# Idle products among the meta queries' values, a reordered norm prologue, and the delta rule's updates by transposes

## The chip, the core and the metric

The kernel runs on one core of a Trainium2 chip. The time is that of one execution on the device, in microseconds (us). The engines are PE (TensorE; PEld is its weight load), DVE (VectorE), ACT (ScalarE), POOL (GpSimd) and SP, which issues most DMAs. Each engine runs its own list of instructions in order; semaphores make one wait for another.

## What is computed

A sequence of 16 meta tokens and 512 real tokens, width 1024, passes through two blocks. In the first block, layer 0 mixes with differential attention (4 heads) and dense attention (8 heads), and layer 1 with windowed attention. The second block drops the meta tokens and has two layers, each with an mLSTM branch, a gated delta rule branch, LayerNorm and a SwiGLU feed-forward part. Of the reference, cut to what the change touches:

```
# block 1, layer 0: the 16 meta queries are a block of their own
o = einsum('bhqs,bhsv->bqhv', softmax(q_meta k) ..., v)

# block 2, delta rule, for each head and chunk of 64 tokens
a_low = where(strict, beta_i * (k_i . k_j) * decay_ij, 0)
u, w  = solve(I + a_low, [v * beta, k * beta * exp(gcum)])

# block 2, layer: LayerNorm over the 1024 features, twice
x = layernorm(alpha * x + mix, ln1_g, ln1_b)
x = layernorm(alpha * x + ffn, ln2_g, ln2_b)
```

## The kernel before, in words

The program is a sequence of stages, each with its own lists for the engines and a barrier behind it. Tokens lie in the free dimension (512 wide), features in the partitions, 8 chunks of 128 features (`KC`). Weights come from HBM in f32 and are split into a rounded high part (ACT, L557) and the remainder (DVE, L690 and, for the first slot in four pieces, L870); the dense products (L441) are made of three products of such parts, all in f32r.

Three places matter here.

**The meta queries' values** (`query_values`, L1208 to L1224, in the attention stage `attA`). When the probabilities of the 16 meta queries have been turned, PE multiplies them with the values in six batches: four of heads whose values are 128 wide, two of pairs of heads 64 wide. Each product has only 16 (or 32) columns. ACT then copies `mix` (L1329), and the ordinary heads go on.

**The norm** (`Normed`, L218 to L309), used five times: at the head of stage `mqkv` in both layers of block 2, at the head of `ffn` in both, and once at the very end (`store`). PE spreads the mean over all partitions (L240), ACT copies it to SBUF (L270), DVE subtracts it from chunk 0 of the activations `h` (L277), POOL from chunks 1 to 7 (L282). DVE scales each chunk (L291), ACT makes its high part (L296), DVE its low part (L299), ACT finishes `h` (L302); PE's first product block (48 products with 512 columns: 8 chunks by 6) follows the chunks as they come. Between the products of the norm PE makes idle ones (`keep_busy`, L101): products of the identity whose result nobody reads, two instructions each. The second weight slot is split while the chunks pass: its high part on ACT after chunk 3, its low part on DVE (L690, 128x2048) after the scale of chunk 5.

The end of a stage that feeds a norm: DVE adds tile 7's residual (L778), adds it to the sum (L753), ACT squares it (L608), DVE adds the squares (L745). PE makes 12 idle products meanwhile (L538), and a barrier ends the stage.

**The delta rule** (`delta_rule`, L2531 is `each`: four products 128x128 in eight instructions; `turn` is four transposes). Two streams (e = 0 and 1) of four heads' chunks run interleaved, in four pairs. The triangular system is inverted by levels b = 1 to 5 with a last quarter-sized one. In a level PE makes y = nb t (bank 0), ACT copies y (L2671), PE makes w = y u (bank 2) and z = uᵀ y (bank 1), and DVE updates both u (L2756, in `room` for stream 0) and its transpose t (L2751). For pairs 0 to 2 the levels also carry pieces of the next pair's preparation (`prepare` on PE, `prepared` on DVE, decays on ACT at L2656 and L2658).

## Time and profile before

| | |
|---|---|
| median of 3 runs | 3865.29 us (3865.06 to 3866.74) |
| the profiled execution: its time, its span | 3866.34 us, 3864.5 us |
| PE busy | 3732.8 us, 97% |
| DVE, ACT, POOL busy | 48%, 31%, 5% |
| mean granted clock of TensorE | 0.98 |

Time and span differ by 1.8 us, which lies around the first and the last instruction. PE is busy nearly always, but "busy" counts idle products, and it counts an instruction's whole time at the lower clock too. In a row of windows each engine has its busy time and its instructions in brackets (PE, PEld, DVE, ACT, POOL), then come TensorE's granted clock as a share of 2.4 GHz, the DMA share and GB/s. In a timeline a row stands for a run of like instructions: start, duration of the run, engine, line, operands, count, and in square brackets the idle time before it and what ended that.

### The profile page before, as it was taken

To read this page: it belongs to the slowest core of one execution; us is meant where nothing else is said; L and a number is where in the kernel's file an instruction comes from. 1 tells how busy PE (TensorE), PEld (TensorE's weight loads), DVE (VectorE), ACT (ScalarE), POOL (GpSimd) and SP (SyncE) were. 2 spreads that over 40 slices of the span, in tenths; PEclk is the share of its full clock that TensorE was granted. 3 is DMA by queue.
4 is the path that set the end of the run, shared out by engine and by line. 5 is a ranking of instruction groups with operands and counts; after the bars stand their busy time and mean duration, and the time that the engine had idled before them with its cause. 6 is when DMAs were issued, how large, how long until landed. Compare 5 with 4: busy or idle time off the path is not lost. (4 is left out here: it accounts for less than half of the span.)

```text
span 3864.5 us, 51800 instructions
## 1 busy us (share of the span) xinstructions
PE 3732.8 (97%) x21089; PEld 3132.3 (81%) x21089; DVE 1860.2 (48%) x2531; ACT 1202.8 (31%) x1762; POOL 197.4 (5%) x216
## 2 busy tenths in 40 slices
PE   8899999999999999999999999999999999999998
PEld 8759999977888787878888788878687788887887
DVE  6475434345534435366554633353536655464334
ACT  3353222244222333232232322234423223323222
POOL 0000000000000100001210100010000122000000
PEclk9899999999999999999999999999999999999999
DMA  3102222212222211220002222221122000222222
GB/s 124 55 2 81 94 88 88 77 54 79 103 90 96 77 55 66 87 87 23 1 28 98 77 92 100 88 82 66 55 97 78 33 1 11 105 77 95 96 91 89
DMA packets 49926, 278.74 MB, mean 72 GB/s; under 512 B 10237, under 2 KB 12797, under 8 KB 20538
## 3 DMA queue, kind: packets, MB, share of 16 engines
q1 hardware_dynamic: 48684, 274.29, 19.8%
q8 instruction: 149, 2.44, 0.2%
q10 hardware_dynamic: 1038, 1.56, 0.1%
q14 instruction: 55, 0.45, 0.0%
HBM read 273.57 MB, written 2.22 MB: 71 GB/s over the span
## 5 line engine op out<-in xcount | busy, mean ns | idle before, releaser
L441 PE MATMUL ps<-xs,ffn_w 128*128 128x512 f32 x2112 | 483.1, 390 | 6.4 <-DVE xs L299 3.8
L441 PEld LDWEIGHTS ps<-xs,ffn_w 128*128 128x128 f32 x2112 | 395.5, 188 | 93.2 <-DVE xs L299 8.4
L441 PE MATMUL ps<-u,mlp_w 128*128 128x264 f32 (+1 forms) x2880 | 454.2, 321 | 0.2 <-DVE u L878 0.2
L441 PEld LDWEIGHTS ps<-u,mlp_w 128*128 128x128 f32 x2880 | 415.9, 189 | 37.6 <-issue 0.3
L441 PE MATMUL ps<-hn,mlp_w 128*128 128x264 f32 (+1 forms) x2304 | 363.6, 320 | 0.0
L441 PEld LDWEIGHTS ps<-hn,mlp_w 128*128 128x128 f32 x2304 | 332.4, 188 | 30.3 <-issue 0.5
L441 PE MATMUL ps<-xs,cv_w 128*128 128x512 f32 x1152 | 268.7, 394 | 0.0
L441 PEld LDWEIGHTS ps<-xs,cv_w 128*128 128x128 f32 x1152 | 215.2, 188 | 59.6 <-issue 13.7
L441 PE MATMUL ps<-ff,ffn_w 128*128 128x512 f32 x1056 | 241.2, 390 | 0.0
L441 PEld LDWEIGHTS ps<-ff,ffn_w 128*128 128x128 f32 x1056 | 198.3, 188 | 41.9 <-issue 1.0
L557 ACT CAST ffn_w<-raw 128x2048 fp32r<-128x2048 f32 (+1 forms) x74 | 124.2, 1678 | 304.0 <-PE ps L441 264.0
L690 DVE TENSOR_TENSOR mlp_w<-raw,mlp_w 128x2048 fp32r<-128x2048 f32 x70 | 160.5, 2292 | 114.7 <-ACT mlp_w L557 114.7
L441 PE MATMUL ps<-hn,qk_w 128*128 128x264 f32 x1344 | 176.7, 294 | 10.2 <-DVE qk L805 10.2
L441 PEld LDWEIGHTS ps<-hn,qk_w 128*128 128x128 f32 x1344 | 172.7, 196 | 13.3 <-issue 12.7
L557 ACT CAST mlp_w<-raw 128x2048 fp32r<-128x2048 f32 x70 | 132.7, 1895 | 155.5 <-PE ps L441 125.4
L441 PE MATMUL ps<-xs,branch_b_w 128*128 128x512 f32 x768 | 180.0, 396 | 0.0
L441 PE MATMUL ps<-xs,branch_a_w 128*128 128x512 f32 x768 | 178.1, 394 | 0.0
L441 PE MATMUL ps<-hbs,branch_b_w 128*128 128x512 f32 x768 | 176.0, 391 | 0.0
L441 PEld LDWEIGHTS ps<-xs,branch_b_w 128*128 128x128 f32 x768 | 146.1, 191 | 32.5 <-issue 2.2
L441 PEld LDWEIGHTS ps<-xs,branch_a_w 128*128 128x128 f32 x768 | 145.3, 189 | 31.8
L441 PEld LDWEIGHTS ps<-hbs,branch_b_w 128*128 128x128 f32 x768 | 144.3, 188 | 30.7 <-issue 1.0
L690 DVE TENSOR_TENSOR ffn_w<-raw,ffn_w 128x2048 fp32r<-128x2048 f32 (+1 forms) x74 | 148.0, 2000 | 41.9 <-ACT ffn_w L557 41.7
(451 smaller groups left out, 5223.0 us busy)
## 6 DMA issues: line engine op xcount, KB each, us to landing
raw<-in_w_ffn_up SPq DMA_DIRECT2D x44, 1024.0 KB, 4.8
raw<-in_w_up SPq DMA_DIRECT2D x32, 1024.0 KB, 4.8
raw<-in_w_down SPq DMA_DIRECT2D x32, 1024.0 KB, 4.7
raw<-in_w_conv SPq DMA_DIRECT2D x24, 1024.0 KB, 4.8
raw<-in_w_ffn_down SPq DMA_DIRECT2D x32, 704.0 KB, 4.1
raw<-in_w_mqk SPq DMA_DIRECT2D x10, 1024.0 KB, 4.8
raw<-in_w_qk_even SPq DMA_DIRECT2D x9, 1024.0 KB, 4.8
raw<-in_w_mv SPq DMA_DIRECT2D x8, 1024.0 KB, 4.8
```

Source lines behind the costliest of these rows:

```text
L441: ins = nc.tensor.matmul(bank(u)[:, h, :], w[:, s, wp, k * g.bw + j * P:k * g.bw + (j + 1) * P], g.xs[:, xp, k, h * n:(h + 1) * n], start= ...
L557: nc.scalar.copy(w[:, s, 0, 0:g.kc * g.bw], ws.raw[:, s, 0:g.kc * g.bw]).then_inc(g.s["high_done"], 1)
L690: nc.vector.tensor_tensor(w[:, s, 1, 0:g.kc * g.bw], ws.raw[:, s, 0:g.kc * g.bw], w[:, s, 0, 0:g.kc * g.bw].bitcast(F32), ALU.subtract).th ...
```

## The change

Eight edits. (1) Normed takes `first`: DVE subtracts the mean from chunks 0 to first-1 and POOL from the rest; first is 3 for the four norms in the layers and 4 for the last. Three idle products between the mean's spread and the wait for `inverted` go. (2) The second slot's high part goes on ACT ahead of chunk 0, its low part on DVE behind chunk 7's low part. (3) At a stage's end with statistics 14 idle products instead of 12. (4) There, ACT's square of tile t waits for one sum fewer. (5) There, DVE adds the square of tile t-1 ahead of its wait for tile t. (6) Two idle products ahead of each of the six batches of `query_values`. (7) In the delta rule the four products z = uᵀy go; PE turns the updated u into the same bank by four transposes, and DVE copies it to t. (8) With it the order within a level: on PE both y, [preparation A], both w, turn A, [preparation B], turn B; on DVE both u, both t, then both prepared pieces.

```diff
--- before.py
+++ after.py
@@ -218,7 +218,9 @@
 
 
 
-    def __init__(self, nc, ps, x, stats, mean, gain, bias, eps, ident):
+
+    def __init__(self, nc, ps, x, stats, mean, gain, bias, eps, ident, first=3):
+        self.first = first
         self.nc, self.ps, self.x, self.stats, self.mean = nc, ps, x, stats, mean
         self.gain, self.bias, self.eps, self.ident = gain, bias, eps, ident
 
@@ -244,7 +246,6 @@
         by_tokens(6, self.stats.sumsq, s["squared"])
         pe.wait_ge(s["m_done"], 1)
         spread(5, self.m, s["m_spread"])
-        keep_busy(nc, ps[:, 3, :], self.ident, 3)
         pe.wait_ge(s["inverted"], 1)
         spread(7, self.r, s["r_spread"])
         keep_busy(nc, ps[:, 3, :], self.ident, 6)
@@ -274,20 +275,22 @@
         dve.wait_ge(s["rooted"], 1)
         nc.vector.reciprocal(self.r[:, :], self.r[:, :]).then_inc(s["inverted"], 1)
         dve.wait_ge(s["m_copied"], 1)
-        nc.vector.tensor_tensor(self.x[:, 0, :], self.x[:, 0, :], self.mean, ALU.subtract).then_inc(s["centred"], 1)
+        for c in range(self.first):
+            nc.vector.tensor_tensor(self.x[:, c, :], self.x[:, c, :], self.mean, ALU.subtract).then_inc(s["centred"], 1)
 
     def gpsimd(self, pool):
         pool.wait_ge(self.s["m_copied"], 1)
-        for c in range(1, KC):
+        for c in range(self.first, KC):
             self.nc.gpsimd.tensor_tensor(self.x[:, c, :], self.x[:, c, :], self.mean, ALU.subtract).then_inc(self.s["centred_p"], 1)
 
     def scale(self, dve, c):
         s = self.s
         if c == 0:
             dve.wait_ge(s["r_spread"], 1)
-            dve.wait_ge(s["centred"], 1)
+        if c < self.first:
+            dve.wait_ge(s["centred"], c + 1)
         else:
-            dve.wait_ge(s["centred_p"], c)
+            dve.wait_ge(s["centred_p"], c - self.first + 1)
         self.nc.vector.scalar_tensor_tensor(self.x[:, c, :], self.x[:, c, :], self.gain[:, c:c + 1], self.ps[:, 7, :],
                                             ALU.mult, ALU.mult).then_inc(s["scaled"], 1)
 
@@ -535,7 +538,7 @@
                 if ws.mat is not None:
                     no = last.t0 + last.tiles + last.extra
                     pe.wait_ge(freed, no + 1)
-                    keep_busy(nc, bank(no % tiles)[:, 0, :], ws.mat, 6 if last.stats is None else 12)
+                    keep_busy(nc, bank(no % tiles)[:, 0, :], ws.mat, 6 if last.stats is None else 14)
 
             @block.scalar
             def _(act):
@@ -604,7 +607,7 @@
                     else:
                         act.wait_ge(freed, tiles + tile_no(g, t, t >= g.tpb) + 1)
                     if t >= 2:
-                        act.wait_ge(g.s["summed"], t - 1)
+                        act.wait_ge(g.s["summed"], max(1, t - 2))
                     nc.scalar.activation(sq[:, t % 2, :], g.dst[:, t, :], ACT.Square).then_inc(g.s["squared"], 1)
 
                 def shift(g):
@@ -653,13 +656,12 @@
                             nc.scalar.activation(sq[:, c % 2, :], whole[:, c, :], ACT.Square).then_inc(x_squared, 1)
                 if normed is not None:
                     normed.roots(act)
+                    high(g, 1, 1)
                     for c in range(KC):
                         normed.high(act, c, g.xs[:, 0, c, :], x_high)
                         if c:
                             act.wait_ge(x_low, c)
                             normed.finish(act, c - 1)
-                        if c == 3:
-                            high(g, 1, 1)
                     act.wait_ge(x_low, KC)
                     normed.finish(act, KC - 1)
                 if beside is not None:
@@ -769,6 +771,8 @@
                 def summed_tile(g, t, pos, j):
                     u, no = slot_of(g, pos, j), tile_no(g, t, t >= g.tpb)
                     shifted = g.stats.shift is not None
+                    if t >= 2:
+                        sum_square(g, t - 1)
                     dve.wait_ge(filled, 1 + no + 1)
                     if shifted and t >= g.tpb:
                         dve.wait_ge(g.s["readied"], t - g.tpb + 1)
@@ -784,8 +788,6 @@
                         add_up(g, t)
                         if t + g.tpb < g.tiles:
                             ready(g, t + g.tpb)
-                    if t >= 2:
-                        sum_square(g, t - 1)
 
                 def tile(g, t, pos, j):
                     u = slot_of(g, pos, j)
@@ -895,9 +897,8 @@
                         normed.scale(dve, c)
                         if c:
                             normed_low(c - 1)
-                        if c == 5:
-                            low(g, 1, 1)
                     normed_low(KC - 1)
+                    low(g, 1, 1)
                 if beside is not None:
                     beside.vector(dve, -1)
                 for i, g in enumerate(gemms):
@@ -1211,6 +1212,7 @@
                     batches += [(n_diff + 2 * g, 2, HD, 1, HD * g, jobs[n_diff + 2 * g][3]) for g in range(2)]
                     for i, count, width, n, col, off in batches:
                         cols = slice(META * i, META * (i + count))
+                        keep_busy(nc, ps[:, 7, 2 * P:4 * P], ident, 2)
                         for j in range(NU + 1):
                             for e in range(1 if diff[i] else 2):
                                 rows = slice(width * e, width * e + width)
@@ -2583,6 +2585,10 @@
                     pe.wait_ge(s["o_copied"], i + 1)
                     nc.tensor.matmul(ps[0:GH, 4 * e + 3, :], pick[:, 2 * i + e, :], f["sq"][:, :], start=True, stop=True).then_inc(s["picked"], 1)
 
+                def turn_update(i, b, e, f, s):
+                    pe.wait_ge(s["u_done"], levels * i + b + 1)
+                    turn(e, 1, f["u"], s["z_filled"])
+
                 for n in range(levels):
                     for e, f, s in both:
                         prepare(0, n, e, f, s)
@@ -2615,9 +2621,12 @@
                                     quarter(e, 2, f["y"], f["u"], s["w_filled"])
                                 else:
                                     each(e, 2, f["y"], f["u"], s["w_filled"])
-                                    each(e, 1, f["u"], f["y"], s["z_filled"])
+                        if 0 < b < levels - 1:
+                            turn_update(i, b, *both[0])
                         if i + 1 < pairs:
                             prepare(i + 1, b, *both[1])
+                        if 0 < b < levels - 1:
+                            turn_update(i, b, *both[1])
                     for e, f, s in both:
                         pe.wait_ge(s["kbe_done"], i + 1)
                         pe.wait_ge(s["u_done"], levels * (i + 1))
@@ -2742,21 +2751,20 @@
                         for e, f, s in both:
                             prepared(i + 1, 0, e, f, s)
                     for b in range(1, levels):
-                        if i + 1 < pairs:
-                            prepared(i + 1, b, *both[0])
                         for e, f, s in both:
                             dve.wait_ge(s["w_filled"], (levels - 1) * i + b)
-                            if b < levels - 1:
-                                dve.wait_ge(s["z_filled"], (levels - 2) * i + b)
-                                nc.vector.tensor_tensor(f["t"][:, :, :], f["t"][:, :, :], bank(e, 1), ALU.subtract).then_inc(s["t_done"], 1)
                             if b == levels - 1:
                                 upper = f["u"][0:HC, :, HC:CHUNK]
                                 ins = nc.vector.tensor_tensor(upper, upper, bank(e, 2)[0:HC, :, HC:CHUNK], ALU.subtract)
                             else:
                                 ins = nc.vector.tensor_tensor(f["u"][:, :, :], f["u"][:, :, :], bank(e, 2), ALU.subtract)
                             ins.then_inc(s["u_done"], 1)
+                        for e, f, s in both if b < levels - 1 else ():
+                            dve.wait_ge(s["z_filled"], (levels - 2) * i + b)
+                            nc.vector.tensor_copy(f["t"][:, :, :], bank(e, 1)).then_inc(s["t_done"], 1)
                         if i + 1 < pairs:
-                            prepared(i + 1, b, *both[1])
+                            for e, f, s in both:
+                                prepared(i + 1, b, e, f, s)
                     for c in range(NCH - 1):
                         for e, f, s in both:
                             dve.wait_ge(s["s_filled"], (NCH - 1) * i + c + 1)
@@ -2776,8 +2784,8 @@
     shifted = Stats(stats.total, stats.sumsq, mean, ones)
     g_rows = sums[0:GH, :, 0:SEQ]
 
-    def normed(gain, bias, eps):
-        return Normed(nc, ps, x, stats, mean, par[:, gain:gain + KC], par[:, bias:bias + KC], par[:, eps:eps + 1], ident)
+    def normed(gain, bias, eps, first=3):
+        return Normed(nc, ps, x, stats, mean, par[:, gain:gain + KC], par[:, bias:bias + KC], par[:, eps:eps + 1], ident, first)
 
     with ExitStack() as ctx:
         with nc.Fori(0, LAYERS2) as layer:
@@ -2835,7 +2843,7 @@
                                           dense("dn1", ff, per // P, D, "add", dst=x, stats=shifted)], whole=x, normed=norm_1,
                       beside=NextParameters(par[:, :], a["par2"][bass.ds(layer + 1, 1), :, :].rearrange("a p n -> (a p) n"), norm_1))
             settle(nc)
-    return normed(IN_G, IN_B, IN_EPS)
+    return normed(IN_G, IN_B, IN_EPS, 4)
 
 
 def second_constants():
```

On PE, in the stage `attA`, at the meta queries' values (`attA_ptq` holds their turned probabilities, `v` the values; `mats` is the identity's tensor). Before:

```order
L1184 MATMUL ps<-mats,attA_prob 128x128 x4
L1136 MATMUL ps<-qk 128x264 x4
L1221 MATMUL ps<-attA_ptq,v 128x16 x4
L1221 MATMUL ps<-attA_ptq_meta,v 128x16
L1221 MATMUL ps<-attA_ptq,v 128x16 x4
L1221 MATMUL ps<-attA_ptq_meta,v 128x16
```

After:

```order
L1185 MATMUL ps<-mats,attA_prob 128x128 x4
L1137 MATMUL ps<-qk 128x264 x4
L101 MATMUL ps<-mats 128x128 x2
L1223 MATMUL ps<-attA_ptq,v 128x16 x4
L1223 MATMUL ps<-attA_ptq_meta,v 128x16
L101 MATMUL ps<-mats 128x128 x2
L1223 MATMUL ps<-attA_ptq,v 128x16 x4
L1223 MATMUL ps<-attA_ptq_meta,v 128x16
```

Two products of 128 columns now stand ahead of each batch of ten instructions (this list counts a product once where the trace has two instructions).

On DVE, in the norm of stage `mqkv` (the stage `ffn` reads alike), before:

```order
L275 RECIPROCAL mqkv_n_r<-mqkv_n_r 128x4
L277 TENSOR_TENSOR h<-h,room 128x512
L870 TENSOR_TENSOR mqkv_w<-raw,mqkv_w 128x512
L291 SCALAR_TENSOR_TENSOR h<-h,room,ps 128x512 x2
L299 SCALAR_TENSOR_TENSOR xs<-h,room,xs 128x512
...
L690 TENSOR_TENSOR mqkv_w<-raw,mqkv_w 128x2048
L291 SCALAR_TENSOR_TENSOR h<-h,room,ps 128x512
L299 SCALAR_TENSOR_TENSOR xs<-h,room,xs 128x512
```

After (both lists leave out scales and low parts of the chunks between, which alternate as those shown):

```order
L276 RECIPROCAL mqkv_n_r<-mqkv_n_r 128x4
L279 TENSOR_TENSOR h<-h,room 128x512 x3
L872 TENSOR_TENSOR mqkv_w<-raw,mqkv_w 128x512
L294 SCALAR_TENSOR_TENSOR h<-h,room,ps 128x512 x2
L302 SCALAR_TENSOR_TENSOR xs<-h,room,xs 128x512
...
L294 SCALAR_TENSOR_TENSOR h<-h,room,ps 128x512
L302 SCALAR_TENSOR_TENSOR xs<-h,room,xs 128x512 x2
L692 TENSOR_TENSOR mqkv_w<-raw,mqkv_w 128x2048
```

Two subtractions have moved ahead of the first scale, and the 128x2048 remainder has moved from among the chunks to behind them.

On PE, in the delta rule, one level of a pair that carries preparation (`room` and `delta_y` are u and y, `delta_t` and `delta_nb` t and nb), before:

```order
L2531 MATMUL ps<-delta_t,delta_nb 128x128 x8
L2549 MATMUL ps<-rows,sel 128x512 x2
L2531 MATMUL ps<-room,delta_y 128x128 x4
L2531 MATMUL ps<-delta_y,room 128x128 x4
L2531 MATMUL ps<-room,delta_y 128x128 x4
L2531 MATMUL ps<-delta_y,room 128x128 x4
L2549 MATMUL ps<-rows,sel 128x512 x2
```

After:

```order
L2533 MATMUL ps<-delta_t,delta_nb 128x128 x8
L2551 MATMUL ps<-rows,sel 128x512 x2
L2533 MATMUL ps<-room,delta_y 128x128 x8
L2546 MATMUL ps<-mats,room 128x128 x4
L2551 MATMUL ps<-rows,sel 128x512 x2
L2546 MATMUL ps<-mats,room 128x128 x4
```

Eight products have become eight transposes, one half ahead of preparation B and one behind it, and the transposes read the u that DVE has just written.

## Rows read from the trace of the kernel before

**Rows 1.** The page's head: busy time and share of the span.
```profile
PE 3732.8 (97%) x21089; PEld 3132.3 (81%) x21089; DVE 1860.2 (48%) x2531; ACT 1202.8 (31%) x1762; POOL 197.4 (5%) x216
```

**Rows 2.** Windows around the meta queries' values.
```profile
174.00:178.00 4.00, 4.00 (x32) 3.35 (x31) 3.21 (x10) 2.08 (x5) 0.20 (x1) 1.00 0.01 1
178.00:180.00 2.00, 2.00 (x14) 1.91 (x14) 0.94 (x2) 0.00 (x0) 0.20 (x1) 0.78 0.74 230
186.00:192.00 6.00, 6.00 (x15) 3.47 (x16) 0.00 (x0) 1.37 (x5) 0.00 (x0) 0.50 0.01 3
```

**Rows 3.** Timeline there: the batches on PE, and what DVE waits for.
```profile
175.52 1.07 PE L1221 MATMUL ps<-attA_ptq,v 128*128 128x16 f32 x8
...
176.84 1.07 PE L1221 MATMUL ps<-attA_ptq,v 128*128 128x16 f32 x8
...
179.68 1.89 PE L1221 MATMUL ps<-attA_ptq,v 128*128 128x16 f32 x8
...
193.88 0.71 DVE L1408 CUSTOM_DVE_ANT_0 attA_prob<-ps,attA_bias 128x528 f32<-128x528 f32 x1 [14.91 <-PE ps L1136]
```

**Rows 4.** Timeline, the norm at the head of `ffn`, first layer of block 2.
```profile
2201.25 0.69 DVE L277 TENSOR_TENSOR h<-h,room 128x512 f32<-128x512 f32 x1 [1.68 <-ACT room L270]
2201.30 6.40 POOL L282 TENSOR_TENSOR h<-h,room 128x512 f32<-128x512 f32 x4 [196.73 <-ACT room L270]
2201.86 1.77 DVE L870 TENSOR_TENSOR ffn_w<-raw,ffn_w 128x512 fp32r<-128x512 f32 x1
...
2203.55 1.39 DVE L291 SCALAR_TENSOR_TENSOR h<-h,room,ps 128x512 f32<-128x512 f32 x2
...
2205.19 1.17 PE L441 MATMUL ps<-xs,ffn_w 128*128 128x512 f32 x4 [0.39 <-ACT xs L296]
```

**Rows 5.** Line L282 over all five norms: duration ns min/median/max.
```profile
L282 POOL TENSOR_TENSOR h<-h,room x35: 1256/1737/1794, 1312.7 to 3858.6; 128x512 f32<-128x512 f32 x35
```

**Rows 6.** Busy time by stretch: end of stage to norm, `ffn`'s first product block, `mqkv`'s.
```profile
2193.00:2196.40 3.40, 0.90 (x9) 0.74 (x8) 1.22 (x2) 1.52 (x4) 0.00 (x0) 1.00 0.00 0
2196.50:2203.00 6.50, 6.50 (x32) 6.50 (x32) 3.50 (x9) 1.78 (x4) 1.70 (x1) 0.50 0.01 3
2205.00:2221.00 16.00, 12.93 (x49) 8.83 (x50) 13.58 (x15) 12.07 (x18) 7.80 (x5) 1.00 0.34 131
1321.00:1336.00 15.00, 15.00 (x53) 9.58 (x52) 9.14 (x11) 10.50 (x15) 3.75 (x3) 1.00 0.20 71
```

**Rows 7.** Timeline of DVE in the last norm, `store`.
```profile
3850.65 0.69 DVE L277 TENSOR_TENSOR h<-h,room 128x512 f32<-128x512 f32 x1 [1.60 <-ACT room L270]
3852.54 2.06 DVE L291 SCALAR_TENSOR_TENSOR h<-h,room,ps 128x512 f32<-128x512 f32 x3 [1.19 <-PE ps L240]
...
3859.89 0.75 DVE L291 SCALAR_TENSOR_TENSOR h<-h,room,ps 128x512 f32<-128x512 f32 x1 [0.48 <-POOL h L282]
```

**Rows 8.** Timeline at the end of the stage ahead of `ffn`.
```profile
2190.39 2.84 PE L101 MATMUL ps<-mats 128*128 128x128 f32 x24
...
2192.71 0.63 ACT L608 ACTIVATE branch_b_tmp<-h 128x512 f32<-128x512 f32 x1 [4.82 <-DVE sums L745]
2193.37 0.69 DVE L745 TENSOR_TENSOR sums<-sums,branch_b_tmp 128x512 f32<-128x512 f32 x1 [0.76 <-ACT branch_b_tmp L608]
```

**Rows 9.** Timeline, delta rule: a level of the last pair.
```profile
1964.41 0.97 PEld L2531 LDWEIGHTS ps<-delta_t,delta_nb 128*128 128x128 f32 x8
...
1966.48 0.97 PEld L2531 LDWEIGHTS ps<-room,delta_y 128*128 128x128 f32 x8
...
1968.65 0.69 DVE L2751 TENSOR_TENSOR delta_t<-delta_t,ps 128x512 f32<-128x512 f32 x1 [2.57 <-PE ps L2531]
...
1970.06 0.97 PEld L2531 LDWEIGHTS ps<-delta_t,delta_nb 128*128 128x128 f32 x8
```

**Rows 10.** Timeline, delta rule: two successive levels of the first pair.
```profile
1805.58 0.52 PEld L2531 LDWEIGHTS ps<-delta_t,delta_nb 128*128 128x128 f32 x4 [0.36 <-issue]
...
1812.63 0.74 PEld L2531 LDWEIGHTS ps<-delta_t,delta_nb 128*128 128x128 f32 x6 [0.36 <-issue]
```

## The prediction

> **What bounds the kernel now.** I read the page's head first: PE is busy 97% of the span and the next engine, DVE, 48% [rows 1]. So a microsecond of PE work that goes is worth one only where PE is really fed at that place, and a microsecond of idle products costs one unless PE would have waited. The page can't tell which, so I went to each place of the change in the timeline and in windows. At the meta queries' values DVE sits idle for 14.91 us, until the product it needs has come through PE's list [rows 3]: there PE alone sets the end, and the granted clock falls from 1.00 to 0.50 (2.4 to 1.2 GHz) on the way [rows 2]. In `mqkv` PE is fully busy behind the norm, 15.00 of 15.00 us, while `ffn`'s first block leaves 3.07 of 16 us idle (12.93 busy) [rows 6]. In the delta rule PE is nearly full too, but its steps hang on one another through DVE and ACT [rows 9]. In the last norm nothing but DVE, POOL and ACT works [rows 7].
>
> **The meta queries' values (edit 6).** Twelve idle products are added where PE sets the end. At a stage's end twelve of them take 2.84 us at full clock [rows 8], so a pair is 0.47 us, and at half clock I take double, as the eight instructions of a batch grow from 1.07 to 1.89 us [rows 3]. The question is whether the clock still falls. Before, it fell in the window from 178 to 180 (0.78 granted: full for some 1.1 us of it, thus until about 179.1), 3.6 us after the first batch had started at 175.52 [rows 2, 3], although PE is counted busy all the time. What PE did were products of 16 columns. The new stretch has 8 instructions of 16 columns, two more, and now four of 128 columns in every 1.32 + 0.47 = 1.79 us; a batch starts every 1.32 us now (175.52, 176.84) [rows 3]. The idle products are a quarter of the time, and between them the array streams as little as before. No row shows such a mixture. I take it that the clock falls at the same time, since three quarters of the stretch are unchanged. Two batches then run at full clock and four at half: 2 x 0.47 + 4 x 0.95 = 4.7, less 0.2 because the clock may come back a little sooner: **+4.5 us**. Bounds: if the clock never fell, the pairs would cost 2.8 and the half-clock stretch would be saved. From 179.1 to some 193 us it is 14 us long, but much of that is PE waiting for ACT or being bound by weight loads; doubling shows as 0.8 us in the eight instructions of a batch [rows 3], and I put the whole saving at about 4.7 us from six such pieces. That bound is -1.9; the other is +5.7, all six pairs at half clock.
>
> **The norm's prologue (edits 1 and 2).** This is the costliest part. In `ffn` DVE subtracts chunk 0 at 2201.25; POOL's first subtraction is queued at 2201.30. DVE's next instruction, L870, has two inputs in SBUF, as the subtraction has. It takes 1.77 us where a subtraction alone takes 0.69 [rows 4], because POOL's instruction went in ahead of it. POOL's own take 1.737 us in the median but 1.256 at best [rows 5]. So the two engines alternate, one instruction each, and each further DVE instruction of this kind costs about 1.72 us as long as POOL has work. DVE was ready at 2201.86, before the end of its own subtraction, and still came second [rows 4]: being next in its own list does not help it. Now three of them stand ahead of the first scale where there was one (L870) behind the subtraction: two more, 2 x 1.72 = 3.44 us. The first scale moves from 2203.55 to about 2206.99, the first product from 2205.19 to about 2208.6. The Trainium skill has this as a rule, in "SBUF — State Buffer", section "SBUF: two separate sides": a DVE instruction with two SBUF inputs and a GpSimd instruction that reads SBUF lock the port pair against each other for the whole instruction, and the other fully blocks. By that rule the change is a loss at this point, and the trace agrees (1.77 against 0.69).
>
> What hides it? In `mqkv` PE is full behind the first chunks, so the delay stands, less some 0.3 us of small waits that vanish: 3.1 us, twice, **+6.2**. In `ffn` the first block's 48 products have 3.07 us of slack (49 instructions by 2221, so the next block starts at about 2220.8) [rows 6]; moreover L690 (2.3 us) leaves the series of chunks. Counted through: scale 0 at +5.74 us from the first subtraction, eight chunks at 1.4 us in the mean (POOL is finished after about five), then 2.3 for L690: the second block may start at +19.6, against 2220.8 - 2201.25 = 19.6 before [rows 4, 6]. That is **+0.3** for both. In the last norm the fourth subtraction ends after 0.69 + 3 x 1.72 = 5.85, eight scales at 0.66 follow, and the last one starts at 3850.65 + 5.8 + 4.6 = 3861.04 instead of 3859.89 [rows 7]: **+1.15**, and ACT's last instruction follows as before. Three idle products less and the earlier spread of `r` are worth nothing, since DVE is now later than `r`. ACT's early high part of slot 1 (1.9 us) lies in ACT's wait for the first scale.
>
> A second cost is the clock. Where PE was busy 0.90 of 3.40 us, the windows behind it show 0.50 [rows 6]. In the new prologue PE has nothing between its last idle product (2204 to 2205) and 2208.6, a gap of about 4 us, where it was under 0.4 [rows 4]. If the clock falls, the first chunks' six products, some 1.4 us a chunk at full clock, take 2.7, against DVE's 1.7 a chunk: 1 us lost on each of one or two chunks. I take 1.5 us for each `mqkv` and 0.5 for each `ffn`, whose slack is partly used: **+4.0**, bounds 0 and +6.
>
> **The delta rule (edits 7 and 8).** The z products of a stream are as long as its w, 1966.48 to 1967.38, 0.90 us, so both streams' are 1.8 us a level [rows 9]. Four transposes are half as many instructions, 0.47 a stream by the 24 that took 2.84 [rows 8]. Were PE the bound without waits, 40 levels (20 per layer, each of both streams) would give 40 x 0.9 = 36 us. But z needs no fresh u: it used y and the old one. The transposes need the new u. The chain of a level of the last pair is then, from w's start: DVE starts on u 1.27 later (as L2751 at 1968.65 behind the products at 1967.38) and takes 0.69 [rows 9]; turn starts about 0.12 after it; the copy of t could start some 0.8 after that (1.27 less half of the eight instructions), but DVE is at the other stream's u until about +2.85; 0.69 for the copy, and with 0.12 again y starts at about +3.65. From y to w it is 1.92 (2.07 in these rows, 1964.41 to 1966.48, of which 0.15 is PE's wait for the other stream's t) [rows 9]. That gives a period of 5.57 us against 1970.06 - 1964.41 = 5.65 [rows 9]: 0.1 saved of 0.9. With preparation the period is 7.05 [rows 10]; there PE has other work in the waits, which is for the change, but the prepared pieces now come behind both t on DVE, the decays on ACT behind them, and ACT's copy of the next y queues behind the decays. Laying the five levels out with these durations I get -0.6, -0.4, +0.7, -0.4, -0.2 and +0.6 at the quarter level, where PE waits for DVE: -0.25 a pair. Three pairs and -0.4 to -0.7 for the last: -1.45 a layer, **-2.9 us** in all. Bounds: -22 us (0.75 saved at each of the 30 prepared levels, if ACT's queue is harmless) and +6 (the wait of +0.7 at two more levels of each of the six prepared pairs would be +8; the last pair's gain off that).
>
> **The stages' ends (edits 3 to 5).** DVE's last sum runs from 2193.37 to 2194.06 and gates the barrier; PE's idle products end at 2193.23 [rows 8]. ACT's last square at 2192.71 waited for the sum before it; freed, it starts about 1.3 us sooner and DVE ends at about 2192.75. But PE now makes 14 idle products and ends at 2193.23 + 0.47 = 2193.70. Gain 0.36 at four ends; at the fifth, ahead of block 2, where other DVE work closes the stage with PE near it, I count 0.3 lost: **-1.1**.
>
> **The sum.** 4.5 + 6.2 + 0.3 + 1.15 + 4.0 - 2.9 - 1.1 = +12.2 on the profiled run's 3866.34 us: 3878.5. The median of the runs shown is 1.05 lower, so the forecast against it is 3877.4, some 0.3% slower.
>
> **The rivals.** What a measurement of this kernel can tell from no change is about 0.2%, 7.7 us: faster is under 3857.6, slower over 3873.0. The forecast's own case, with the clock in the norms' gaps at its bounds (+8 to +14), gives 3873 to 3880: chance 0.58, of which 0.06 falls below 3873.
>
> (A) DVE keeps its turn over consecutive subtractions, and POOL comes only after them. Then scale 0 comes at about +2.5 instead of +2.3, POOL has fewer chunks to do, and L690's stall in `ffn` goes: at most 3.07 us in each `ffn`, I count 2.5, and 1.5 in `store`, nothing in `mqkv`. The norms give -6.5 instead of +11.65, the sum is -6.0, 3859.3. For it: nothing but that POOL's wait here ended 0.05 after DVE's. Against: L870 is just such a consecutive instruction and lost its turn [rows 4]. 0.08.
>
> (B) The idle products hold the clock at the meta queries' values: -1.9 instead of +4.5, 3871.0, just inside no change. For it: they are the only wide products there. 0.12.
>
> (C) The delta rule follows PE's work, not the chain: -22 instead of -2.9 gives 3858, with a little more or with (B) it is faster than 3857.6. This is the rival on the other side. It decides once a prepared level is shorter than 7.05 by over 0.75 us. For it: PE is nearly full there; against: the chain of the last pair, which is 5.57 by the same rows. 0.12.
>
> (D) The delta rule gets slower by the queue of decays on ACT, +6: 3886. 0.10.
>
> Slower: 0.52 + 0.01 + 0.04 + 0.10 = 0.67, lowered to 0.63 as several small terms are estimates; faster 0.03 from (A), 0.07 from (C): 0.10; the same 0.27. The range from 3860 to 3885 leaves out (D)'s end and the larger half of (C).
>
> **What would show it.** In the norms: two of the three L279 at about 1.7 us instead of 0.69, the first L441 of each norm 3.4 us later against the first subtraction, a granted clock under 1.00 just behind it; if the subtractions take 0.69 each, (A) holds. At the meta queries: L101 pairs of 0.47 and then 0.95 us, and the window around 186 to 192 still at 0.50; at 1.00, (B) holds. In the delta rule: y of one level to y of the next, 5.6 and about 7.0 us; 6.3 speaks for (C). At the ends: L608's last square right behind L778, and the barrier behind PE. The prediction is wrong above all if PE's work sets the delta rule's pace, or if the alternation with POOL is another thing than I read.

## The result, and the profile after

The changed kernel takes 3876.6 us (median of 8 runs, 3872.5 to 3880.49) against 3866.15 us of the kernel before (8 runs, 3864.14 to 3870.77): ratio 1.0027, interval [1.0017, 1.0036]. It is slower by 0.27%; the forecast was 3877.4 us, 0.3%. The profiled execution took 3879.14 us with a span of 3877.3, 12.8 us longer than before's.

PE is counted less busy than before [rows 1], since the delta rule lost products, and yet the span is longer. The page's head after:

```profile
PE 3725.1 (96%) x20783; PEld 3114.4 (80%) x20783; DVE 1875.2 (48%) x2542; ACT 1201.0 (31%) x1762; POOL 181.0 (5%) x205
```

**The meta queries' values.** Windows, then the timeline of the same place:

```profile
174.00:178.00 4.00, 3.75 (x28) 3.13 (x29) 3.36 (x10) 1.96 (x5) 0.20 (x1) 1.00 0.00 0
178.00:180.00 2.00, 2.00 (x18) 1.94 (x17) 1.16 (x3) 0.12 (x2) 0.20 (x1) 0.96 0.74 197
186.00:192.00 6.00, 4.99 (x49) 4.25 (x49) 0.00 (x0) 1.32 (x11) 0.00 (x0) 0.50 0.01 3
```

```profile
179.44 0.91 PE L101 MATMUL ps<-mats 128*128 128x128 f32 x4
180.15 1.73 PE L1223 MATMUL ps<-attA_ptq,v 128*128 128x16 f32 x8
...
182.34 1.22 PE L101 MATMUL ps<-mats 128*128 128x128 f32 x4
...
198.92 0.71 DVE L1410 CUSTOM_DVE_ANT_0 attA_prob<-ps,attA_bias 128x528 f32<-128x528 f32 x1 [19.54 <-PE ps L1137]
```

The reader sees the clock fall at the third pair, as it fell in the third to fourth batch before [rows 2, 3], and the later pairs at half clock (1.22 us with the last one's end). DVE's work starts at 198.92 where it started at 193.88: 5.0 us later. Of this 0.4 us was there ahead of the batches: counted from the products of `attA_prob` in front of them (on PE, L1184 at 173.85 before, L1185 at 174.25 after), the stretch takes 24.7 us instead of 20.0, so the edit costs 4.6 us. In the nine further traces that have no idle products here the stretch takes 20.1 us six times and 18.5 us three times.

**The norm**, in `ffn` of the first layer, to set against [rows 4]; behind it the line of the moved subtractions over all norms:

```profile
2206.98 4.05 DVE L279 TENSOR_TENSOR h<-h,room 128x512 f32<-128x512 f32 x3 [1.68 <-ACT room L271]
2207.02 8.04 POOL L284 TENSOR_TENSOR h<-h,room 128x512 f32<-128x512 f32 x5 [195.98 <-ACT room L271]
...
2210.95 1.75 DVE L872 TENSOR_TENSOR ffn_w<-raw,ffn_w 128x512 fp32r<-128x512 f32 x1
2212.62 1.39 DVE L294 SCALAR_TENSOR_TENSOR h<-h,room,ps 128x512 f32<-128x512 f32 x2
...
2214.26 1.19 PE L444 MATMUL ps<-xs,ffn_w 128*128 128x512 f32 x2 [5.16 <-ACT xs L299]
```

```profile
L279 DVE TENSOR_TENSOR h<-h,room x16: 693/1746/1779, 1321.3 to 3866.3; 128x512 f32<-128x512 f32 x16
```

Three subtractions take 4.05 us, the first 0.69 and the others 1.75. The first scale stands 5.64 us behind the first subtraction, where it was 2.30 [rows 4]. PE waits 5.16 us for its first product, and the granted clock falls on top: 0.81 from 2203.9 to 2213.

**The last norm**, DVE, against [rows 7]:

```profile
3862.35 5.71 DVE L279 TENSOR_TENSOR h<-h,room 128x512 f32<-128x512 f32 x4 [1.83 <-ACT room L271]
3867.98 5.34 DVE L294 SCALAR_TENSOR_TENSOR h<-h,room,ps 128x512 f32<-128x512 f32 x8
```

From the first subtraction to the end of the last scale it is 10.97 us now, and 3860.64 - 3850.65 = 9.99 before: +1.0.

**The end of a stage**, against [rows 8]:

```profile
2197.39 3.29 PE L101 MATMUL ps<-mats 128*128 128x128 f32 x28
...
2198.32 0.63 ACT L611 ACTIVATE branch_b_tmp<-h 128x512 f32<-128x512 f32 x1 [4.82 <-DVE h L782]
2198.32 0.69 DVE L755 TENSOR_TENSOR sums<-sums,h 128x512 f32<-128x512 f32 x1
2198.98 0.69 DVE L747 TENSOR_TENSOR sums<-sums,branch_b_tmp 128x512 f32<-128x512 f32 x1
```

ACT's square starts right behind the residual; DVE is through at 2199.67, and now PE's idle products, until 2200.68, gate the barrier.

**The delta rule**, a level of the last pair, against [rows 9]:

```profile
1972.83 2.02 PE L2533 MATMUL ps<-delta_t,delta_nb 128*128 128x128 f32 x16
...
1974.69 2.00 PE L2533 MATMUL ps<-room,delta_y 128*128 128x128 f32 x16
...
1976.57 0.66 PE L2546 MATMUL ps<-mats,room 128*128 128x128 f32 x4
...
1978.16 2.02 PE L2533 MATMUL ps<-delta_t,delta_nb 128*128 128x128 f32 x16
```

The period is 5.33 us (before 5.65).

In a pair that carries preparation the starts of y on PE are now 6.31, 6.42, 7.57, 6.56 and 5.77 us apart (before 7.05, 7.05, 7.25, 7.15 and 6.33; the fifth step leads to the quarter-sized level). In the long one PE waits for ACT's copy of y, which stands behind the decays on ACT. In the quarter-sized level (its y at 1895.87) it waits for DVE:

```profile
1879.77 2.05 PE L2533 MATMUL ps<-room,delta_y 128*128 128x128 f32 x16 [0.41 <-ACT delta_y L2680]
...
1895.87 0.67 PE L2541 MATMUL ps<-delta_t,delta_big_n 64*64 64x64 f32 x8
...
1897.99 0.63 PE L2546 MATMUL ps<-mats,qkv 128*128 128x128 f32 x4 [0.61 <-DVE qkv L2725]
...
1900.12 1.95 PE L2533 MATMUL ps<-room,qkv 128*128 128x128 f32 x16
```

The same level before, in the second layer:

```profile
3156.70 1.16 PE L2539 MATMUL ps<-delta_t,delta_big_n 64*64 64x64 f32 x16
...
3159.99 2.02 PE L2531 MATMUL ps<-room,qkv 128*128 128x128 f32 x16
```

**Where the 12.8 us arose.** Starts of the same work on PE in the two traces, and how much later each is after the change:

| mark | before | after | later by |
|---|---|---|---|
| behind the meta queries' values | 192.34 | 197.57 | 5.2 |
| first scores of layer 1's attention, block 1 | 812.41 | 817.28 | 4.9 |
| norm of `mqkv` | 1309.12 | 1317.44 | 8.3 |
| second product block of `mqkv` | 1335.33 | 1348.52 | 13.2 |
| `branch_a` | 1483.37 | 1493.53 | 10.1 |
| delta rule | 1773.55 | 1784.16 | 10.6 |
| `branch_b` | 2008.75 | 2015.23 | 6.5 |
| norm of `ffn` | 2195.72 | 2202.32 | 6.6 |
| `ffn`, way down | 2329.60 | 2335.69 | 6.1 |
| norm of `mqkv`, layer 2 | 2580.59 | 2586.79 | 6.2 |
| past `mqkv`, layer 2 | 2642.50 | 2652.40 | 9.9 |
| delta rule, layer 2 | 3043.14 | 3055.43 | 12.3 |
| `branch_b`, layer 2 | 3278.21 | 3288.94 | 10.7 |
| last norm | 3846.36 | 3856.21 | 9.8 |
| end | 3864.5 | 3877.3 | 12.8 |

Most steps are those of the forecast, but three are not, all in stages that nothing touches: +3.4 us between 812 and 1309, -3.1 ahead of the first `branch_a`, and +2.4 between `mqkv` and the delta rule of layer 2. The first of these places in windows, after and (last row) before:

```profile
908.00:914.00 6.00, 5.51 (x32) 3.19 (x34) 0.51 (x3) 0.58 (x1) 0.00 (x0) 0.72 0.01 3
914.00:922.00 8.00, 5.62 (x27) 4.58 (x22) 5.77 (x10) 5.73 (x12) 0.10 (x1) 0.79 0.00 0
```

```profile
908.00:915.00 7.00, 4.87 (x26) 4.14 (x27) 5.26 (x10) 5.61 (x11) 0.10 (x1) 1.00 0.00 0
```

PE's work is the same; the granted clock isn't. The runs that follow ask whether that is chance.

### The profile page after: what moved, and what is told of

Same layout as the page of the kernel before. It is cut to its first block and busy times, and to the rows that moved or that the text cites. A ratio compares the mean times of both kernels' runs of the same rounds, so it can differ in the third digit from the quotient of the medians.

```text
span 3877.3 us, 51108 instructions
## 1 busy us (share of the span) xinstructions
PE 3725.1 (96%) x20783; PEld 3114.4 (80%) x20783; DVE 1875.2 (48%) x2542; ACT 1201.0 (31%) x1762; POOL 181.0 (5%) x205
## 3 DMA queue, kind: packets, MB, share of 16 engines
q8 instruction: 147, 2.41, 0.3%
## 5 line engine op out<-in xcount | busy, mean ns | idle before, releaser
L856 DVE TENSOR_TENSOR ffn_res<-ffn_tmp,ps 128x512 f32<-128x512 f32 x44 | 30.3, 689 | 280.3 <-PE ps L444 276.1
```

The costliest lines, as they stand in the source:

```text
L856: nc.vector.tensor_tensor(res[:, v, :, :], tmp[:, v, :, :], bank(slot_of(g, pos, 1)), ALU.mult).then_inc(freed, 2)
```

## The experiments

All ratios are to runs of the kernel before on the same chip. The experiments ran on several chips, where the median of the kernel before was 3865.97 to 3869.45 us, so two experiments are compared by their ratios. Where a figure is given by stage, it is the difference of starts in the traces, as in the table above.

**1. The changed kernel without the idle products** (edit 6 undone).

```diff
-                        keep_busy(nc, ps[:, 7, 2 * P:4 * P], ident, 2)
```

> The changed kernel without the idle products among the meta queries' values (edit 6 undone). In the traces of before and after, DVE's first work behind these values starts at 193.88 and at 198.92 us: 5.0 us later with the change. If the idle products alone did that, the start is back at 193.9 within 0.3 us, the granted clock between 180 and 192 is 0.50 as before, and the whole is 5 us faster than the changed kernel, about 3872. Rival: another edit or the run moved it, and the start stays near 199.

3868.17 us (10 runs), ratio 1.0004 [0.9995, 1.0014]. PE's work behind the values starts at 192.66 (before 192.34, after 197.57). So the idle products are the 5 us there. But the whole is 8.4 us under the change's median (by the ratios 9), more than the 5 expected: the 3.4 us between 812 and 1309 are gone too (0.2 in this trace).

**2. The further subtractions alone** on the kernel before.

```diff
-        nc.vector.tensor_tensor(self.x[:, 0, :], self.x[:, 0, :], self.mean, ALU.subtract).then_inc(s["centred"], 1)
+        for c in range(self.first):
+            nc.vector.tensor_tensor(self.x[:, c, :], self.x[:, c, :], self.mean, ALU.subtract).then_inc(s["centred"], 1)
...
-        for c in range(1, KC):
+        for c in range(self.first, KC):
```

> The kernel before with the two (in the last norm three) further subtractions on DVE and nothing else: the idle products of the norm and the place of the second slot's split stay as they were. Forecast's theory, alternation with POOL: two of three subtractions take about 1.7 us, the first product of each norm comes 3.4 us later against the first subtraction, and the whole is slower by more than the change's own norms were, since L690 still stands among the chunks: mqkv +4 each, ffn +3 each, store +1.2, so +13 to +17, about 3881. Rival (A), DVE keeps its turn: subtractions of 0.69 us each and no more than +2. A third theory: the second slot's place is worth nothing, then ffn is within 1 us of before and the whole is +10.

3883.98 us (4 runs), ratio 1.0045 [1.0028, 1.0062]: slower than the change as a whole. First products 3.3 us late in `mqkv` and in `ffn`, and of these `ffn` keeps 2.5 by its way down. What holds it is the 128x2048 split still in the midst of the chunks, in DVE's timeline:

```profile
2217.91 0.75 DVE L303 SCALAR_TENSOR_TENSOR xs<-h,room,xs 128x512 fp32r<-128x512 f32 x1 [1.23 <-ACT xs L300]
2218.58 2.28 DVE L694 TENSOR_TENSOR ffn_w<-raw,ffn_w 128x2048 fp32r<-128x2048 f32 x1
2220.78 0.74 DVE L295 SCALAR_TENSOR_TENSOR h<-h,room,ps 128x512 f32<-128x512 f32 x1
```

**3. The delta rule's change alone** (edits 7 and 8).

> The kernel before with the delta rule's change alone (edits 7 and 8). In the trace after, each prepared pair is 1.3 us shorter than before wherever the clock was the same, and a level of the last pair 0.31 us. Theory 1, the chain through u, the turn and t sets the level: the same figures, so 5 to 6 us a layer where no clock fall comes in between, and 3855 to 3860 for the whole. Theory 2, the lighter work of PE lets the clock fall more often in the delta rule (after: 3.4 us at half clock in several places where before had one), and it takes the gain back: more windows below 1.00 than before in both layers, and a whole of 3862 to 3866. Theory 3, PE's work sets the pace: 0.9 us per level, 3830.

3863.24 us (10 runs), ratio 0.9989 [0.998, 0.9999]. The time is in theory 2's range; against this chip's kernel before, 3867.91, it is 4.7 us less, between theories 1 and 2. The first layer gives 1.4 us, the second 4.4, and from the second level of a pair on the levels are the same in both: the starts of y follow one another by 6.43, 7.57, 6.56 and 5.77 us where they did by 7.05, 7.25, 7.15 and 6.33. Theory 3 (PE's work) is out.

What differs between the layers is the clock, at the pairs' ends and in their first levels. From the quarter-sized level to the next pair's first y it is 19.75 us at full clock and 21.3 with a fall (18.85 before); the first level of a pair grows by 1.6 or 3.1 us where the clock falls in it. In this trace the falls make 6.2 us in the first layer and 3.1 in the second, where a layer of the kernel before has 1.6. Three windows of this kernel: inside the first pair's first level, a pair's end in the second layer with a fall, and one without:

```profile
1796.00:1799.00 3.00, 3.00 (x11) 2.12 (x11) 0.00 (x0) 0.59 (x1) 1.44 (x2) 0.50 0.02 5
3096.00:3118.00 22.00, 19.84 (x147) 16.18 (x146) 12.85 (x24) 5.91 (x16) 5.05 (x4) 0.92 0.00 1
3204.00:3222.00 18.00, 16.73 (x142) 14.07 (x142) 10.56 (x20) 5.91 (x16) 4.54 (x4) 1.00 0.00 1
```

Put together from pieces at full clock alone (an estimate), a layer takes 182.7 us from the first y to the last quarter-sized level, against 188.2 before: 5.4 us less. So each theory has its share: the chain gives theory 1's 5 to 6 us a layer, and theory 2's falls take part of it back.

**4. The stages' ends alone** (edits 3 to 5).

> The kernel before with the stages' ends alone (edits 3 to 5: 14 idle products, ACT's square and DVE's sum freed of one another). Theory: at four ends DVE is finished 1.3 us sooner and PE's idle products, 0.45 us longer, now gate the barrier, so each end gives 0.4 us, the fifth loses 0.3: -1.3 in all, no change that the times can tell (3863 to 3867). Rival: DVE still gates, and nothing moves at all. Second rival: the barrier waits for something else (ACT or a DMA), then the next stage's first instruction stands where it did although DVE and PE ended otherwise.

3866.05 us (10 runs), ratio 0.9999 [0.9989, 1.0008]: no difference that the times tell. By stage: -0.4, -0.1, -0.4 and -0.3 at the four ends, as computed for all but one. Neither rival holds where the 0.4 is seen; the end with -0.1 doesn't tell.

**5. The change without its two losing parts**: no idle products among the values, one subtraction on DVE as before; the second slot's move, the ends and the delta rule as changed.

> The changed kernel without its two losing parts: no idle products among the meta queries' values, and the mean subtracted from chunk 0 alone on DVE, as before (the norm's three idle products stand too). The second slot's place, the stages' ends and the delta rule are as changed. From the other traces, stage by stage: delta rule alone -4.4 us a layer where the clock is the same (-8.8, of which falls of the clock took 3 in the first layer), the ends -0.4 each (-1.2), and in ffn, where the further subtractions without the second slot's move ended at -0.8 behind a first product at +3.3, and with it at -3.0 behind +2.6, the move gives about 2 to 2.5 each. Sum -12 to -14: 3854 to 3858 against 3867.9. Rival: the move of the second slot is worth something only behind a delayed start (DVE then has the slot's split hidden anyway), so -8 to -10.

3854.01 us (6 runs), ratio 0.9967 [0.9955, 0.9979]: 0.33% faster than before, 12.0 us at the medians, at the near edge of the -12 to -14 expected. `ffn` gives 2.0 us in each layer without any subtraction moved, so the rival (the move pays only behind a late start) is out. In DVE's timeline the split stands behind the last chunk, and PE no longer waits for it:

```profile
2211.93 1.62 DVE L299 SCALAR_TENSOR_TENSOR xs<-h,room,xs 128x512 fp32r<-128x512 f32 x2
2213.47 2.28 DVE L689 TENSOR_TENSOR ffn_w<-raw,ffn_w 128x2048 fp32r<-128x2048 f32 x1
```

**6 and 7. Three and four idle products** ahead of each batch, in the kernel before.

```diff
+                        keep_busy(nc, ps[:, 7, 2 * P:4 * P], ident, 3)
```

> The kernel before with three idle products ahead of each of the six batches instead of none. At full clock they are 18 x 0.223 = 4.0 us. Forecast's theory, the clock falls as long as the narrow products take most of the time: with three wide ones in some 2 us of a batch it still falls, and the first ordinary work of DVE behind the values starts 7 us later than before. Rival (B) in a milder form: three are enough, the granted clock stays at 1.00 through the batches, and the start is within 1 us of before (+4.0 for the products, -4.7 for the stretch at half clock).

> The same with four: 24 x 0.223 = 5.4 us at full clock. If the clock now holds, DVE's first ordinary work behind the values starts at about +0.7 against before, and the windows from 180 to 188 show 1.00. If it falls all the same, at +9 to +10. With two (the change) it fell and the start was at +5.0.

Three: 3871.52 us (8 runs), ratio 1.001 [1.0, 1.002]; the window from 180 to 184 has a granted clock of 0.54, and DVE starts at 202.32, 8.4 us late (7.6 counted from the products ahead of the batches). Four: 3876.01 us (8 runs, 3866.79 to 3881.52), ratio 1.0024 [1.0013, 1.0035]. In its trace, one of the faster executions, the clock stands at full speed through the batches and falls behind them:

```profile
180.00:184.00 4.00, 4.00 (x36) 3.92 (x35) 0.00 (x0) 0.00 (x0) 0.00 (x0) 1.00 0.01 4
184.00:186.00 2.00, 2.00 (x30) 1.81 (x30) 0.00 (x0) 0.00 (x0) 0.00 (x0) 1.00 0.00 0
186.00:192.00 6.00, 4.99 (x36) 2.83 (x35) 0.00 (x0) 2.13 (x12) 0.00 (x0) 0.79 0.00 0
```

DVE starts at 197.09, 3.2 us late instead of 0.7 (3.4 counted from the products ahead of the batches): behind the batches, where PE waits 1.0 us for ACT's `mix`, the clock falls after all. So enough idle products can hold the clock through the batches, and it doesn't pay. This is shown for one execution alone. The other seven spread from 3866.79 to 3881.52, four of them over 3878, and the median is 10 us above this chip's kernel before; whether the clock held in those isn't shown.

**8. One idle product ahead of each wait for the updated u**, on the delta change alone.

```diff
                 def turn_update(i, b, e, f, s):
+                    keep_busy(nc, bank(e, 1)[:, 0, :], ident, 1)
                     pe.wait_ge(s["u_done"], levels * i + b + 1)
```

> The kernel before with the delta rule's change and one idle product ahead of each wait for the updated u (80 a layer's pair of streams all told, 160 in the kernel of 0.22 us), where PE waits 0.2 to 0.45 us anyway. It tells whether the half-clock stretches in the delta rule after the change come from PE's lighter work. Theory 2: they vanish (none in the prepared pairs of either layer) and both layers show -4 against before, 3860 or a little under. Rival: the stretches stand as they are, since the waits are only half filled, and every idle product that is longer than its wait costs: 0 to -2 against before. Third: the idle products never fit, the chain grows by 0.1 us a level, and it is slower than the delta change alone by 4.

3865.42 us (10 runs), ratio 0.9997 [0.9988, 1.0006]; the delta change alone has 0.9989, about 3 us less, but the intervals overlap. The windows from 1830 to 1970, first of this kernel, then of the delta change alone:

```profile
1830.00:1970.00 140.00, 133.87 (x1070) 117.41 (x1069) 80.46 (x133) 38.62 (x92) 40.50 (x33) 1.00 0.00 1
```

```profile
1830.00:1970.00 140.00, 132.81 (x1026) 114.73 (x1025) 80.65 (x135) 39.35 (x94) 42.82 (x34) 0.98 0.00 1
```

The clock now holds, as theory 2 said: neither layer has a fall between its first y and its last quarter-sized level. But a prepared level takes 6.80 us instead of 6.43, and a layer gains only 2.0 to 2.2. The lighter load is what lets the clock fall, for with PE's waits filled all falls are gone. Filling costs 5.6 us a layer (188.3 us against the 182.7 at full clock of experiment 3). The falls that it removes make 1.6 to 6.4 us in the sixteen layers of the eight other traces with this change, 4.7 in the mean: some 1 us less than the filling.

**9. No POOL in the norm**: experiment 1's kernel, with the later subtractions on DVE too, each just ahead of its scale.

```diff
-        for c in range(self.first, KC):
+        for c in range(self.first, KC) if not self.own else ():
...
+        if self.own and c >= self.first:
+            self.nc.vector.tensor_tensor(self.x[:, c, :], self.x[:, c, :], self.mean, ALU.subtract).then_inc(s["centred"], 1)
```

> The changed kernel without the idle products among the meta queries' values (as in the run that undid edit 6), and with all of the mean's subtractions on DVE: the first three (four) in a row as in the change, each later one just ahead of its chunk's scale. POOL does none. It tells whether the 1.7 us a subtraction are the two engines' alternation. Theory: with POOL silent each subtraction takes 0.69 and L872's last piece too, the first scale starts 2.6 us behind the first subtraction instead of 5.7, and the first product of the norm comes at +0.3 against before instead of +3.3 in mqkv. A chunk on DVE is then subtraction, scale and low part, about 1.95 us, less than the 2.25 of PE in mqkv, so mqkv ends at about before's time; in ffn (1.36 us of PE a chunk) DVE sets the pace. Whole: about 3 to 4 us a mqkv less than its sister's 3868.2, so some 3861. Rival: the subtractions are slow for another reason (the length of the list, an operand's place), and stay at 1.7.

3856.98 us (5 runs), ratio 0.9969 [0.9956, 0.9982]; its sister, experiment 1, has 1.0004. That is 11 us at the medians and 13 to 14 by the ratios, more than expected: `mqkv` takes 1.0 us less than before in each layer, where the sister takes 4.9 and 3.7 more. DVE's timeline in `mqkv`:

```profile
1311.38 1.90 DVE L279 TENSOR_TENSOR h<-h,room 128x512 f32<-128x512 f32 x3 [0.72 <-ACT room L271]
1313.19 0.69 DVE L874 TENSOR_TENSOR mqkv_w<-raw,mqkv_w 128x512 fp32r<-128x512 f32 x1
1313.79 1.40 DVE L296 SCALAR_TENSOR_TENSOR h<-h,room,ps 128x512 f32<-128x512 f32 x2
```

The same three subtractions in the same list take 1.90 us instead of 4.05, and the first scale comes after 2.41 us instead of 5.6. This settles it: what made them slow is POOL's own work, not their place.

**10. `mqkv` alone without POOL**, on the kernel of experiment 5, one subtraction ahead.

> The kernel of the run without first and idle products (3854.0, the fastest so far), and in mqkv's norms alone every subtraction on DVE, one ahead of the first scale and each later one ahead of its own. Theory: L870's last piece takes 0.69 instead of 1.77, the first product starts 1.1 us sooner and PE, which is full behind it, passes that on: -1.1 in each mqkv, 3852. Rival: a chunk of 1.95 us on DVE is too slow when PE asks for one in 1.4 (the gates' products come only with the second chunk), and the gain is lost again by the third chunk: no difference.

3854.61 us (6 runs, 3844.81 to 3859.69), ratio 0.9968 [0.9956, 0.998]: no difference to experiment 5, but in the first layer not for the rival's reason. DVE was through early and then waited for PE's spread of r, which stands behind the norm's three idle products:

```profile
1313.40 0.75 DVE L297 SCALAR_TENSOR_TENSOR h<-h,room,ps 128x512 f32<-128x512 f32 x1 [1.06 <-PE ps L242]
```

The traced execution is the fastest of all here, 3844.81 us, 9.8 us under its kernel's median. Against experiment 5's trace it gains 4 us between `mqkv` and the first delta rule and 5.8 in that delta rule, where the two kernels are the same and the falls of the clock are not.

**11. The same without those idle products in `mqkv`.**

> The kernel of the run in which mqkv's subtractions are all on DVE, without the norm's three idle products there. In that run the first scale waited 1.06 us for PE's spread of r, which came behind the idle products at half clock, so the last piece's faster end brought nothing: the median stayed at 3854.6 against 3854.0. Theory: with them gone (they stay in ffn and store) the spread comes about 0.9 us sooner and the first scale 1.1 us behind its former place, the first product of mqkv at -1.1 against the kernel before, passed on in full: 1 us each layer, 3852.5. Rival: PE's longer idle stretch costs as much by the clock, and the median stays at 3854.

3853.69 us (6 runs), ratio 0.9965 [0.9953, 0.9977]. The first scale stands at 1311.38, 1.40 us behind the subtraction at 1309.98. Per stage `mqkv` gives 1.0 and 1.2 us, but the median is within a microsecond of experiment 5's: the mechanism is shown, the gain in time is not.

**12. The changed kernel once more.**

> The changed kernel once more, unchanged. In its first trace some 3.3 us arose between 818 and 922 us, in stages that the change does not touch, with granted clocks of 0.81 and 0.90 where the other traces show 1.00 but for one short stretch. If these fall by where an execution happens to stand, the second trace has them elsewhere or not at all, and the stages touched show the same differences as in the first: +5 at the meta queries' values, +3.3 at each first product of mqkv. If the shift of 5 us at the meta queries' values brings them on, the second trace shows them again.

3877.64 us (6 runs), ratio 1.0025 [1.0013, 1.0037]. Between 812 and 1309 the second trace again shows +3.5 us, with falls of the clock at the same two places. The kernels whose work stands there at before's time or up to 3.0 us earlier show 0.0 to 0.4, and the one with three idle products, which stands there 8.4 us later, shows 0.3. So it isn't chance from run to run: both traces with a shift of 4.9 and 6.3 us at this place have these falls, and none of the eleven traces of other kernels has the loss. As far as these traces tell, it isn't the size of the shift that costs but where it sets the later stages. Which moment decides was not tried.

## Why the prediction was right

**The meta queries' values.** Forecast +4.5, measured 5.0 at DVE's start, of which 0.4 was there before: 4.6 in both traces of the changed kernel, with two pairs at full clock and four at half. Rival (B), that the idle products hold the clock, is out for two and three products a batch. With four its mechanism is true, in the one trace, but its price is not: it still costs 3.4 us. The price of the edit is over 8 us all the same: to the 5.0 on the spot come 3.4 in untouched stages, which the forecast did not have.

**The norm's prologue.** The reading that POOL and DVE alternate stood: 1.75 us a subtraction (forecast 1.72), first product +3.3 us (3.4), +4.9 and +3.7 us for the two `mqkv` with the clock (4.6 each), and experiment 9 took the cause away. Rival (A) is out: it gave 3859.3 and 0.69 us a subtraction. The rule of the Trainium skill ("SBUF — State Buffer", "SBUF: two separate sides"), that a DVE instruction with two SBUF inputs and a GpSimd instruction that reads SBUF lock each other out for the whole instruction, agrees with 1.75 us here and 0.69 with POOL silent.

In `ffn` the sum was mis-sized: +0.3 and +1.0 for the clock in both together, measured -0.6 (-0.5 and -0.1) in the profiled pair, and -0.5 and +1.2 in the changed kernel's second trace. The terms that I wrote down, 5.74 + 8 x 1.4 + 2.3, add up to 19.2 and not to 19.6. The move of the split gives back all of the delay, though PE starts 2.5 and 2.8 us late against the stage's own start. By itself that move is worth 2.0 us a layer (experiment 5), which I had used up against the delay and not named as a gain of its own.

In the last norm +1.15 was forecast; the profiled pair has +3.0 from its start to the end, of which the norm on DVE is 1.0. The other 1.9 us arise ahead of the first subtraction, which stands 4.28 us behind the stage's start before and 6.14 after, with a granted clock of 0.90 and 0.50 in the first 2 us. This part moves from trace to trace, from 4.06 to 6.14 us: experiments 3 and 4, whose last norm is that of before, have 6.13 and 6.14, experiment 5 has 4.61, and the changed kernel's second trace 4.66. So it is the state of the clock at that moment and not the change; the change's part is +1.0.

**The delta rule.** The chain sets the pace, as forecast, and not PE's work: rival (C) needed over 0.75 us a prepared level, and the five levels of a pair give 0.4 in the mean. The size was off: -2.9 forecast, -4.1 and -1.6 in the two layers of the profiled pair, and 2.4 to 11.0 us gained in both layers together over the eight traces with this change, which differ chiefly by falls of the clock. The step that was mis-sized is my laying out of the levels: I had -0.6, -0.4, +0.7, -0.4, -0.2 and +0.6 for a pair, -0.3 in all; the trace has -0.7, -0.6, +0.3, -0.6, -0.6 and +0.9 up to the next pair, -1.3 in all. The two losses are of the kinds that I named. The wait for ACT behind the decays is there (0.41 us in the line above), but the level loses 0.3 and not 0.7. The quarter-sized level does wait for DVE: from its y to the products of the updated u PE takes 4.25 us instead of 3.29, which is the whole of the +0.9. What I had too small is the gain of the other levels. In the last pair the turn starts 1.88 us behind w, where I had 2.08. Rival (D) is out; but the falls of the clock, a mechanism of neither, took 3.1 to 6.2 us of a layer's gain in the profiled run, where a layer of before has 1.6.

**The stages' ends.** -1.1 forecast. Alone (experiment 4) the four ends give 0.4, 0.1, 0.4 and 0.3 us, as laid out. In the profiled pair they are +0.1, +0.1, -0.3 and -0.4: too small for one pair of traces to tell.

**The sum.** 12.2 us forecast, 12.8 in the profiled pair, 10.5 at the medians. That it is so near is luck, for errors cancel: the delta rule, `ffn` and `mqkv` came out some 5 us better than forecast, the last norm and the ends 2.4 us worse, and the untouched stages, which the forecast had at nothing, gave +3.4, -3.1, +0.5 and +2.4 us. The sign, and the order of the costs, rest on steps that the runs confirmed.

## What to carry to other kernels

Before part of the work is moved from POOL to DVE, look whether DVE's instructions read two inputs in SBUF while POOL still works on its own: here a 0.69 us instruction cost 1.75 next to POOL, so the way to a sooner start was to silence POOL (experiment 9), not to share with it. Idle products paid at neither place that was tried: two or three a batch did not hold the clock, four did in the one trace and still cost 3.4 us, and in the delta rule they removed the falls for slightly more than these cost. And a change of several parts is best taken apart: without its two losing parts this one is 0.33% faster than before.

## What the runs showed of the hardware that was not expected

A delay of 5 us at one place made the granted clock fall at two other places 700 us later, in both traces of the changed kernel, and cost another 3.4 us; a delay of 8.4 us, in its one trace, did not. Elsewhere too the falls come and go. In the delta rule they cost 1.6 us apiece (19.75 against 21.3 us at a pair's end), and two layers of one execution that do the same work differ by about 3 us in four of the eight traces with the unfilled change. Stages that no kernel here touches differ by up to 3 us between traces in this way (from the second product block of `mqkv` to `branch_a`: +0.1 us against before in experiment 5, -1.4 in experiment 3 and -3.1 in the changed kernel). A kernel's own runs, where there are five or more, spread over 5 to 15 us, and this sets what a single profile can tell of a term: differences by stage under 2 us are to be believed only where both traces show the same clock.
